# Delta-rule scan: the unit-triangular inverse on 32-row blocks in four diagonal tiles of the array, with two product steps joining them

## The reference, cut to what matters

```python
def _gdn_chunked(q, k, v, g, beta, s0):          # per head: q, k of width 64, v of width 64
    ...
    gdiff = gc[..., :, None] - gc[..., None, :]
    decay = jnp.where(incl, jnp.exp(jnp.where(incl, gdiff, 0.0)), 0.0)
    kb = kc * bc
    lower = jnp.where(strict, jnp.einsum('nbhid,nbhjd->nbhij', kb, kc) * decay, 0.0)
    a_mat = lower + jnp.eye(GDN_CHUNK, dtype=f32)
    rhs = jnp.concatenate([vc * bc, kb * jnp.exp(gc)[..., None]], axis=-1)
    sol = lax.linalg.triangular_solve(a_mat, rhs, left_side=True, lower=True, unit_diagonal=True)
    u, w = sol[..., :dv], sol[..., dv:]
    ...
    def step(state, xs):                          # sequential over the chunks
        v_new = u_i - jnp.einsum('bhck,bhkv->bhcv', w_i, state)
        o_i = (jnp.einsum('bhck,bhkv->bhcv', q_i * jnp.exp(g_i)[..., None], state)
               + jnp.einsum('bhij,bhjv->bhiv', a_i, v_new))
        state = state * decay_of_chunk + jnp.einsum('bhck,bhcv->bhkv', k_scaled, v_new)
```

## Time and profile before

| | us |
|---|---|
| median of 3 runs | 3024.26 |
| lowest and highest | 3023.71, 3024.54 |
| the profiled execution, its own time | 3019.77 |
| span of the profile (first to last instruction) | 3018.2 |

### The profile page before, as it was taken

The page is one execution under the profiler, slowest core; times in us unless marked ns, Lnnn a source line. Parts: engine busy times, 40 slices in busy tenths (PEclk is TensorE's granted clock), DMA queues, the critical chain, the costliest instruction groups (busy, mean ns, idle before and its releaser), DMA issues.

```text
span 3018.2 us, 55846 instructions
## 1 busy us (share of the span) xinstructions
PE 2843.2 (94%) x23136; PEld 2384.0 (79%) x23136; DVE 1061.4 (35%) x1944; ACT 798.2 (26%) x1214; POOL 659.2 (22%) x428
## 2 busy tenths in 40 slices
PE   6999999999999899999989998999999998999997
PEld 3558855887778899999956697568777888999997
DVE  1546613236533411111344474132465233111113
ACT  2131013223321422122221411232233214221222
POOL 0002101221222233333301110021122222333332
PEclk9999999999999999999999999999999999999998
DMA  7110011222124222223330100112221332322222
GB/s 307 35 47 13 3 37 42 81 79 79 64 99 137 80 92 91 92 84 93 98 129 22 43 4 6 59 49 79 79 79 64 128 105 87 98 85 92 88 95 77
DMA packets 56672, 235.54 MB, mean 78 GB/s; under 512 B 6625, under 2 KB 6785, under 8 KB 55137
## 3 DMA queue, kind: packets, MB, share of 16 engines
q1 hardware_dynamic: 53568, 206.67, 20.8%
q0 software_dynamic: 2848, 25.13, 2.2%
HBM read 222.96 MB, written 8.81 MB: 77 GB/s over the span
## 4 chain that ended last, share of the span: by engine, by line
PE 87%; issue 4%; DVE 3%; ACT 3%; POOL 1%; DMA 1%; SPq 0%; POOLq 0%; DVEq 0%; ACTq 0%
PE ps_dense L774 43%; PE ps_dense L767 14%; PE ps_aux L774 4%; PE ps_aux L1350 3%; PE ps_dense L1299 3%; PE ps_aux L1096 2%; PE ps_aux L1076 2%; PE ps_aux L1088 2%; PE ps_aux L1299 1%; PE ps_dense L1376 1%; PE ps_dense L1364 1%; DMA w_ring<-in_w_early 1%; PE ps_dense L797 1%; PE ps_aux L797 1%; POOL w_low L679 1%
## 5 line engine op out<-in xcount | busy, mean ns | idle before, releaser
L679 POOL TENSOR_TENSOR w_low<-w_ring,w_high 128x1024 fp32r<-128x1024 f32 x208 | 512.5, 2465 | 1226.3 <-ACT w_high L1613 1226.3
L774 PE MATMUL ps_dense<-h_high,w_high 128*128 128x320 f32 x2048 | 482.6, 317 | 52.8 <-DVE h_low L2029 22.2
L774 PE MATMUL ps_dense<-h_low,w_high 128*128 128x320 f32 x2048 | 469.0, 310 | 0.0
L774 PE MATMUL ps_dense<-h_high,w_low 128*128 128x320 f32 x2048 | 468.9, 310 | 0.0
L767 PE MATMUL ps_dense<-h_norm,w_ring 128*128 128x512 f32 (+1 forms) x1536 | 432.1, 442 | 18.7 <-ACT h_norm L1638 10.7
L767 PEld LDWEIGHTS ps_dense<-h_norm,w_ring 128*128 128x128 f32 x1536 | 239.1, 195 | 216.3 <-issue 205.2
L774 PEld LDWEIGHTS ps_dense<-h_high,w_high 128*128 128x128 f32 x2048 | 339.5, 189 | 67.7 <-issue 29.9
L1613 ACT ACTIVATE w_high<-w_ring 128x1024 fp32r<-128x1024 f32 x208 | 219.4, 1056 | 569.8 <-PE ps_dense L774 350.6
L774 PEld LDWEIGHTS ps_dense<-h_low,w_high 128*128 128x128 f32 x2048 | 345.0, 189 | 0.0
L774 PEld LDWEIGHTS ps_dense<-h_high,w_low 128*128 128x128 f32 x2048 | 344.8, 189 | 0.0
L774 PE MATMUL ps_dense<-z_high,w_high 128*128 128x320 f32 x1024 | 235.6, 311 | 0.0
(11 more groups left out here) (404 smaller groups left out, 3557.5 us busy)
## 6 DMA issues: line engine op xcount, KB each, us to landing
w_ring<-in_w_mlp SPq DMA_DIRECT2D x128, 512.0 KB, 3.7
w_ring<-in_w_gate SPq DMA_DIRECT2D x64, 640.0 KB, 4.0
w_ring<-in_w_late SPq DMA_DIRECT2D x64, 512.0 KB, 4.7
w_ring<-in_w_early SPq DMA_DIRECT2D x48, 512.0 KB, 3.6
w_ring<-in_w_in SPq DMA_DIRECT2D x48, 512.0 KB, 3.6
w_ring<-in_w_out SPq DMA_DIRECT2D x16, 512.0 KB, 3.7
arena<-in_dft POOLq DMA_DIRECT2D x2, 3264.0 KB, 12.9
par<-in_par POOLq DMA_DIRECT2D x3, 1731.0 KB, 7.6
```

The lines of the kernel that those rows point to most:

```text
L679: g.tensor_tensor(w_low[:, n % 2], ring[:, slot, 0:KC, :], w_high[:, n % 2].bitcast(F32), ALU.subtract).then_inc(w_low_in.sem, 1)
L774: last = mm(out[:, s, 0:HALF], w_[:, par_, k, :], x_[:, k, s * HALF:(s + 1) * HALF], start=k == 0 and x_ is x_high and w_ is w_high, stop= ...
```

## The change

Levels 0 to 4 now work on four diagonal 32x32 blocks of each unit. Each of the three product groups of a level has 32 products of 32x32x32 in four diagonal tiles of the array (`quarter(q)`), where it had 16 of 64x64x64 in two. The buffers `xi`, `xt`, `wm` are 32 wide, so each DVE operation of a level covers 128x256 elements instead of 128x512. The masks and the identity in the constants shrink with them.

Level 5 is replaced. `joint_lower` forms L21·X11 for each 64-block (16 products of 32x32x32 in off-diagonal tiles). ACT `sides_in` copies it to SBUF without a mask. `joint_inverse` forms the off-diagonal block of X (8 products, only the blocks that the corner step reads) and of its transpose (16 products). The DVE operations of level 5 go away. ACT takes the assembling over, in a new function `joints`: `half_diagonal` (4 copies of 32 partitions x 128 elements per chunk), `half_side` (2), `turned_diagonal` (4) and `turned_sides` (4) put the 32-blocks into the 64-wide buffer `xd` and into `xtf`. POOL clears `xd` once a layer. The corner steps read `xd` and `wd` instead of `xi` and `wm`.

```diff
@@ constants
-    ("eps", 1), ("eps4", 1), ("sel", 8), ("ones", 128), ("ident", 128), ("blk", 128), ("tri", 256), ("maskt", 256), ("identc", 64),
-    ("lvlc", 6 * 128), ("rot", 128), ("cos", LAT), ("sin", LAT), ("wf", 5), ("alt", 1), ("altrow", LAT), ("pick", 16),
+    ("eps", 1), ("eps4", 1), ("sel", 8), ("ones", 128), ("ident", 128), ("blk", 128), ("tri", 256), ("maskt", 256), ("eye", 32),
+    ("lvlc", 5 * 64), ("rot", 128), ("cos", LAT), ("sin", LAT), ("wf", 5), ("alt", 1), ("altrow", LAT), ("pick", 16),
@@ gdn buffers
-        xi, xt, wm = ([cv(8, 64) for _ in range(2)] for _ in range(3))
+        xi, xt, wm = ([cv(8, 32) for _ in range(2)] for _ in range(3))
+        xd, wd = ([cv(4, 64) for _ in range(2)] for _ in range(2))
+        wp = [cv(4, 32) for _ in range(2)]
@@ POOL
                 for i in range(2):
-                    last = g.memset(xtf[i], 0.0)
+                    g.memset(xtf[i], 0.0)
+                    last = g.memset(xd[i], 0.0)
@@ PE, lower_times (inverse_times changes in the same way)
-                        for r in range(2):
-                            mv = xi[i][rows(r), u] if k else c_("identc", rows(r))
-                            last = mm(psA[rows(r), 2 * i, u * 64:(u + 1) * 64], lt[s % 3][rows(r), d, hh, rows(r)], mv,
-                                      start=True, stop=True)
+                        for q in range(4):
+                            mv = xi[i][quarter(q), u] if k else c_("eye", quarter(q))
+                            last = mm(psA[quarter(q), 2 * i, u * 32:(u + 1) * 32],
+                                      lt[s % 3][quarter(q), d, hh, quarter(q)], mv, start=True, stop=True)
@@ PE, new
+                def joint_lower(s):
+                    i = s % 2
+                    held(pe, *xi_in[i].nth(l, turn_no(s, 6, 5)))
+                    for hh in range(H):
+                        for d in range(2):
+                            for r in range(2):
+                                src, dst = quarter(2 * r + d), quarter(2 * r + 1 - d)
+                                last = mm(psA[dst, 2 * i, hh * 32:(hh + 1) * 32], lt[s % 3][src, d, hh, dst],
+                                          xi[i][src, d * 4 + hh], start=True, stop=True)
+                    last.then_inc(w_ps[i].sem, 1)
+                def joint_inverse(s):
+                    i = s % 2
+                    held(pe, *wm_in[i].nth(l, turn_no(s, 6, 6)))
+                    held(pe, *xt_in[i].nth(l, turn_no(s, 6, 5)))
+                    for hh in range(H):
+                        for d in range(2):
+                            dst = quarter(1 + d)
+                            last = mm(psA[dst, 2 * i, P + hh * 32:P + (hh + 1) * 32], xt[i][dst, d * 4 + hh],
+                                      wp[i][dst, hh], start=True, stop=True)
+                    last.then_inc(xi_ps[i].sem, 1)
+                    for hh in range(H):
+                        for d in range(2):
+                            for r in range(2):
+                                src, dst = quarter(2 * r + d), quarter(2 * r + 1 - d)
+                                last = mm(psA[src, 2 * i + 1, hh * 32:(hh + 1) * 32], wp[i][dst, hh],
+                                          xt[i][dst, d * 4 + hh], start=True, stop=True)
+                    last.then_inc(xt_ps[i].sem, 1)
@@ PE, the order (the same for chunks 2, 3 and for chunk 4)
-                lower_times(0, 5)
-                lower_times(1, 5)
-                inverse_times(0, 5)
-                inverse_times(1, 5)
+                joint_lower(0)
+                joint_lower(1)
+                joint_inverse(0)
+                joint_inverse(1)
                 keys_of_state(0)
                 corner_lower(0)
@@ ACT, new
+                def sides_in(s):
+                    act.wait_ge(*w_ps[i].nth(l, s // 2 * 7 + 6))
+                    a(wp[i], psA[:, 2 * i, 0:P].rearrange("p (h j) -> p h j", h=H), ACT.Copy).then_inc(wm_in[i].sem, 1)
+                def half_diagonal(s):
+                    act.wait_ge(*xi_in[i].nth(l, s // 2 * 6 + 5))
+                    for d in range(2):
+                        for b in range(2):
+                            lanes = quarter(2 * d + b)
+                            a(xd[i][lanes, :, 32 * b:32 * b + 32], xi[i][lanes, d * 4:d * 4 + 4], ACT.Copy)
+                def half_side(s):
+                    act.wait_ge(*xi_ps[i].nth(l, s // 2 * 5 + 5))
+                    for d in range(2):
+                        lanes = quarter(1 + d)
+                        src = psA[lanes, 2 * i, P:2 * P].rearrange("p (h j) -> p h j", h=H)
+                        last = a(xd[i][lanes, :, 32 * d:32 * d + 32], src, ACT.Copy, scale=-1.0)
+                    last.then_inc(xi_in[i].sem, 1)
+                def turned_diagonal(s):
+                    act.wait_ge(*xt_in[i].nth(l, s // 2 * 6 + 5))
+                    if s >= 2:
+                        act.wait_ge(*vn_ps.nth(l, s - 1))
+                    for q in range(4):
+                        lanes = quarter(q)
+                        a(xtf[i].rearrange("p d h j -> p (d h) j")[lanes, :, lanes], xt[i][lanes], ACT.Copy)
+                def turned_sides(s):
+                    act.wait_ge(*xt_ps[i].nth(l, s // 2 * 7 + 6))
+                    for d in range(2):
+                        for r in range(2):
+                            lanes, cols = quarter(2 * r + d), quarter(2 * r + 1 - d)
+                            src = psA[lanes, 2 * i + 1, 0:P].rearrange("p (h j) -> p h j", h=H)
+                            last = a(xtf[i][lanes, d, :, cols], src, ACT.Copy, scale=-1.0)
+                    last.then_inc(xt_in[i].sem, 1)
+                def joints(*chunks):
+                    for s in chunks:
+                        half_diagonal(s)
+                        sides_in(s)
+                    for s in chunks:
+                        half_side(s)
+                        turned_diagonal(s)
+                        turned_sides(s)
+                    for s in chunks:
+                        corner_in(s)
+                    for s in chunks:
+                        corner_out(s)
@@ DVE: w_masked, inverse_less, turned_less on 32-wide units; the calls of k = 5 are gone
-                                    psA[:, 2 * i, :].rearrange("p (d h j) -> p d h j", d=2, h=H),
-                                    masks[:, k].unsqueeze(2).to_broadcast([P, 2, H, 64]), ALU.mult)\
+                                    psA[:, 2 * i, 0:256].rearrange("p (d h j) -> p d h j", d=2, h=H),
+                                    masks[:, k].unsqueeze(2).to_broadcast([P, 2, H, 32]), ALU.mult)\
```

More of the change, by code:

```diff
@@ L1086, in inverse_times @@
                         for u in range(8):
-                            for r in range(2):
-                                last = mm(psA[rows(r), 2 * i, u * 64:(u + 1) * 64], xt[i][rows(r), u], wm[i][rows(r), u],
-                                          start=True, stop=True)
+                            for q in range(4):
+                                last = mm(psA[quarter(q), 2 * i, u * 32:(u + 1) * 32], xt[i][quarter(q), u],
+                                          wm[i][quarter(q), u], start=True, stop=True)
                         last.then_inc(xi_ps[i].sem, 1)
@@ L1093, in inverse_times @@
                     for u in range(8):
[L1094 to L1096 removed]
+                        for q in range(4):
+                            mv = xt[i][quarter(q), u] if k else c_("eye", quarter(q))
+                            last = mm(psA[quarter(q), 2 * i + 1, u * 32:(u + 1) * 32], wm[i][quarter(q), u], mv,
                                       start=True, stop=True)
+                    last.then_inc(xt_ps[i].sem, 1)
[25 more added lines that the diff above has]
+                                          xt[i][dst, d * 4 + hh], start=True, stop=True)
                     last.then_inc(xt_ps[i].sem, 1)
@@ L1252, in gdn @@
                 inverse_times(3, 4)
-                lower_times(2, 5)
-                lower_times(3, 5)
+                joint_lower(2)
+                joint_lower(3)
                 keys_of_state(2)
-                inverse_times(2, 5)
-                inverse_times(3, 5)
+                joint_inverse(2)
+                joint_inverse(3)
                 corner_lower(2)
@@ L1277, in gdn @@
                 inverse_times(4, 4)
-                lower_times(4, 5)
-                inverse_times(4, 5)
+                joint_lower(4)
+                joint_inverse(4)
                 corner_lower(4)
@@ L1774, in gdn @@
                 decay_exp(3)
-                corner_in(0)
-                corner_in(1)
-                act.wait_ge(*xtf_zero.nth(l, 1))
-                corner_out(0)
-                corner_out(1)
+                joints(0, 1)
                 values_in(0)
@@ L1782, in gdn @@
                 decay_exp(4)
-                corner_in(2)
-                corner_in(3)
-                corner_out(2)
-                corner_out(3)
+                joints(2, 3)
```

(9 more changed lines are left out.)

53 lines of the change are left out of this document (20 added, 33 removed).

## The result

The changed kernel takes 3115.98 us (median of 4 runs, 3113.48 to 3118.94), the kernel before 3023.99 (4 runs): ratio 1.0307, 95% interval [1.0295, 1.0319]. It is 3% slower where 1.8% faster was predicted, and 102 us above the predicted range.

A forecast was written before the change was run, and what follows sets the result against it. PE was taken to bound A to D, latency from PE to DVE and back E. Gains of 10.1 + 0.8 + 9.3 + 0.2 + 6.0 = 26.4 us a layer, 52.8 in both, gave 2971 us, range 2950 to 3014.

The forecast's parts named there:

- The product groups: Levels 0 to 4: a group of 64 records in four tiles takes 0.53 us instead of 0.94.
- rival 2: Only two tiles overlap or 7 ns an instruction; packets 1.2 us each; group stays 0.9 us; 3016 us; chance 0.11.
- A: Stretch of levels 0 to 4 of chunks 0, 1: from 38.2 to 28.1 us, a gain of 10.1.
- Clock in E: Chunk 4: 0.6 us taken off the gain for PE's slower clock with more idle time.
- E: Stretch of chunk 4, 46.2 us, paced by latency from PE to DVE and back: a gain of 6.0 us.
- Granted clock still 1.00 in A and C: Sign expected in the changed profile: PE keeps its full clock in levels 0 to 4 of chunks 0 to 3.
- C: Stretch of levels 0 to 4 of chunks 2, 3 with two scan steps: from 45.2 to 35.9 us, gain 9.3.
- Joints: Level 5 and corners: ACT the new bound, 30 copies at 0.27 us = 8.1, starting 0.4 us before `joint_lower`.
- B: First stretch of level 5 and corners: from 11.1 to 10.3 us, a gain of 0.8.
- D: Second stretch of level 5 and corners: from 10.2 to 10.0 us, a gain of 0.2.
- The other terms: Rest of the stretch forecasts, A 28.1, C 35.9, E 40.2 us, with DVE level operations at 0.42 us.
- Rival 1: One floor for all tiles: records of different tiles start no closer than 27 to 29 ns; 3128 us; chance 0.11.

The follow-up runs named there:

- wider: Changed kernel with only every fourth unit's level products kept, each covering four units' columns (32 instructions a group): 2986.9 us, ratio 0.988.
- wider_warm: wider plus products nobody reads, put into PE's idle time in stretch E: 2960.3 us, ratio 0.9796.
- probe: Kernel before with blocks of extra small products and a loop of them behind the scan, results unread: 3277.22 us.
- wide: Changed kernel with every second unit's level products left out, each remaining one covering two units' columns (64 instructions a group): 2989.8 us, ratio 0.9879.

## Why the prediction was wrong, step by step

Per layer the prediction had 124.5 us for the stage and the kernel after took 195.9. The runs split the 71.4:

- **Supply of instructions, with the clock that falls in its pauses: 62.0 us** (after 195.9, wider 133.9; up to 7 us of it are wider's shorter groups, 70 x 0.10). The step that failed is in "The product groups": it took the columns as the only limit of a group, noted that no row shows the rate per instruction at 4.1 ns, and put the risk into rival 2 with 0.11. A group itself does run in 0.54 us. But the average over A had to be 7.3 ns an instruction, and 13.5 to 15 is what comes.
- **The sizing of that rival.** It priced a packet at the 1.2 us that it lasts, as if they followed one another at once. The packets of after stand 3.5 to 4.3 us apart in A, at 2.1% of the DMA engines' time in the window shown: the length of a transfer isn't its period. The rows had a warning. The old stream gives 14.6 ns an instruction within a group, and no row shows a denser one sustained; that hardly more could be had was not seen. With 256 instructions per 3.5 us, A's 3,850 instructions are 53 us where A took 38.2 before, and the sign of the forecast turns.
- **Clock in E: 7.7 us** (wider against wider_warm). The prediction took off 0.6 us for it. "Granted clock still 1.00 in A and C" is wrong as well: 0.76 and 0.85.
- **Joints: 6.5 us** (B and D of wider_warm 13.4 each for 10.3 and 10.0). The copies of a chunk sum to 4 x 0.307 + 0.278 + 2 x 0.268 + 4 x 0.414 + 4 x 0.268 = 4.8 us in place of 4.05, 1.4 us for a pair of chunks; `turned_diagonal` was sized at half of its elements. In B the other large part is the start: the first copy was forecast 0.4 us ahead of `joint_lower` and starts 1.1 us behind it, after an exponential of 1.06 us that stands before it in ACT's list. In D it starts 0.1 us ahead. There `corner_inverse` takes 1.97 us for 1.15 in B and the `lower_times` behind it 1.07 for 0.64, both at the slower clock. Half a microsecond of D stays unexplained. That ACT becomes the bound there was right: it is busy 12.0 and 11.6 of the 13.4 us.
- **The other terms: 4.8 us better than forecast** with these three set aside: A 25.9 for 28.1, C 35.2 for 35.9, E 38.3 for 40.2 (E of wider_warm). Wider's groups of 0.44 us for the 0.53 of the forecast are 28 x 0.09 = 2.5 us of that in A and as much in C, so that these terms were about right. DVE's 0.42 us and the distance of groups were right, and so was the reading that four tiles run side by side.

Rival 1 gave 3128, near the 3116 measured, and is nevertheless wrong: records of different tiles start 8 to 9 ns apart. The number alone would have picked the wrong mechanism; the pauses in the timeline and the probe tell them apart. Of the Trainium skill's rule that start to start never falls below about 25 ns (TensorE: Matmul & The Clock Gate, "Wait — 56ns, not 53.3ns?"), the runs leave only what it says of one tile: across four tiles the probe has 8 to 9 ns. Another of its pages (Runtime: NRT & Kernel Launch, "Instruction fetch mechanics") says that instructions come in blocks of 256 and that crossing to the next one is mostly hidden. The first half agrees with the probe, which stops every 256 instructions; the second doesn't hold for a stream of small matmuls, which waited 1.4 to 2.1 us at each.

## What to carry to other kernels

Before cutting matmuls into smaller tiles, divide the instructions of the stretch (loads and matmuls, over hundreds of them) by the time that is hoped for, and compare with the densest stream that the traces show as sustained; here that is 13.5 to 15 ns an instruction, while a short burst or a loop runs at 4 to 8. A resource's period has to be read between two of its uses, not from the length of one. And where a change leaves PE idle on the path, price what runs after it at the lower clock, for it cost 7.7 us of a 46 us stretch here. Last, look at the loops behind the place that was changed: the MLP's changed by 5 us a layer though no edit touched it.

## What the runs showed of the hardware that was not expected

- Instructions reach PE in blocks of 256, one per 3.45 to 3.7 us in the probe; it runs some 400 beyond slow work before it first pauses, and a loop of 64 instructions, 16 turns, runs without any of these waits at 8 ns an instruction.
- Much longer loops can stay in store: the one of the MLP, 1,668 recorded loads and matmuls a turn, took no packet in turns 2 to 4 in six kernels and some nine a turn in the others, 115.9 us against 117.3 to 117.9.
- Four 32x32 tiles at 8 columns start a record every 8 to 9 ns, and a record with its load costs two instructions, about 4 ns each.
- With pauses of up to 2.3 us that recur, A of after has a granted clock of 0.76, and the same stretch with half the instructions (wide) 1.00. Products that nobody reads, put into idle time, made E 7.7 us shorter.
